# A hybrid decoder layer: softmax row factors of attention taken from TensorE transposes to a DMA round trip

## What is computed

```python
logits = where(mask, scores * 64 ** -0.5 + F[t] - F[s], -inf)
p = softmax(logits, axis=-1)          # row sum over the keys
out = einsum('bhqk,bkhd->bqhd', p, v)
```

## Time and profile before

| | |
|---|---|
| median of 3 runs | 1952.44 us (1950.23 to 1953.33) |
| profiled execution, its own time | 1954.57 us |
| its span | 1953.0 us, mean granted TensorE clock 0.994 |
| TensorE matmuls | 1915.2 us busy, 98% |
| TensorE weight loads | 1624.5 us, 83% |
| VectorE | 1124.6 us, 58% |
| ScalarE | 709.0 us, 36% |
| GpSimd | 435.1 us, 22% |
| DMA | 221.69 MB, mean 114 GB/s |

### The profile page before, as it was taken

The page is one execution under the profiler, slowest core; times in us unless marked ns, Lnnn a source line. Parts: engine busy times, 40 slices in busy tenths (PEclk is TensorE's granted clock), DMA queues, the critical chain, the costliest instruction groups (busy, mean ns, idle before and its releaser), DMA issues. The chain is left out here.

```text
span 1953.0 us, 30551 instructions
## 1 busy us (share of the span) xinstructions
PE 1915.2 (98%) x10560; PEld 1624.5 (83%) x10560; DVE 1124.6 (58%) x2142; ACT 709.0 (36%) x1090; POOL 435.1 (22%) x548
## 2 busy tenths in 40 slices
PE   8999999999999999999999999999999989999998
PEld 6878887888887888888888788888888878999997
DVE  5564235654244655646566665565655568777676
ACT  3121013021034554555555655455555541111110
POOL 2927940498000000000000000000000002222322
PEclk9999999999999999999999999999999999999999
DMA  7124225322432141241513515133142276555642
GB/s 191 67 88 118 86 86 194 65 108 107 131 118 94 49 129 63 71 120 48 138 57 91 182 50 139 56 88 109 48 136 66 88 258 215 165 173 170 173 118 87
DMA packets 104568, 221.69 MB, mean 114 GB/s; under 512 B 11000, under 2 KB 56744, under 8 KB 100904
## 3 DMA queue, kind: packets, MB, share of 16 engines
q1 hardware_dynamic: 90736, 161.41, 26.2%
q0 software_dynamic: 12608, 55.19, 10.3%
q10 hardware_dynamic: 1152, 4.19, 0.5%
HBM read 155.09 MB, written 65.08 MB: 113 GB/s over the span
## 5 line engine op out<-in xcount | busy, mean ns | idle before, releaser
L1441 PE MATMUL g_ps<-x_hi,w_lo 128*128 128x512 f32 x768 | 310.2, 404 | 0.0
L1441 PE MATMUL g_ps<-x_hi,w_hi 128*128 128x512 f32 x768 | 308.7, 402 | 0.0
L1355 DVE TENSOR_TENSOR pt_lo<-t_ps,pt_hi 128x512 fp32r<-128x512 f32 (+2 forms) x320 | 191.7, 607 | 133.9 <-ACT pt_hi L1263 132.1
L1441 PE MATMUL g_ps<-x_lo,w_hi 128*128 128x512 f32 x768 | 228.4, 411 | 4.0 <-PEq L1478 2.6
L695 PE MATMUL tile_ps<-x_hi,w_hi 128*128 128x512 f32 x736 | 228.4, 391 | 0.0
L695 PE MATMUL tile_ps<-x_lo,w_hi 128*128 128x512 f32 x736 | 226.7, 389 | 0.0
L695 PE MATMUL tile_ps<-x_hi,w_lo 128*128 128x512 f32 x736 | 226.6, 389 | 0.0
L1263 ACT ACTIVATE pt_hi<-t_ps 128x512 fp32r<-128x512 f32 (+2 forms) x320 | 170.4, 534 | 134.3 <-PE t_ps L1400 129.4
L1171 POOL DMA_DIRECT2D mixT<-y_out x63 | 33.8, 536 | 749.7 <-DVE y_out L1309 749.7
L1295 DVE CUSTOM_DVE_ANT_0 s_sb<-s_ps,f_row 128x512 f32<-128x512 f32 (+2 forms) x320 | 180.6, 604 | 18.6 <-PE s_ps L1389 17.9
L1400 PE MATMUL t_ps<-ident,s_sb 128*128 128x128 f32 x1088 | 171.7, 273 | 0.9 <-DVE pt_lo L1355 0.9
(11 more groups left out here) (288 smaller groups left out, 3574.0 us busy)
## 6 DMA issues: line engine op xcount, KB each, us to landing
w_lo_raw<-in_w_tiles SPq DMA_DIRECT2D x96, 512.0 KB, 3.6
gateT<-g_out SPq DMA_DIRECT2D x96, 256.0 KB, 3.0
gate<-gateT SPq DMA_DIRECT2D x64, 384.0 KB, 4.6
qkvT<-zout SPq DMA_DIRECT2D x24, 512.0 KB, 3.2
x_lo_raw<-in_xT SPq DMA_DIRECT2D x20, 512.0 KB, 8.6
silT<-zout SPq DMA_DIRECT2D x16, 512.0 KB, 2.6
k_ll<-qkvT POOLq DMA_DIRECT2D x16, 512.0 KB, 7.2
q_st<-qkvT POOLq DMA_DIRECT2D x16, 512.0 KB, 8.9
```

The lines of the kernel that those rows point to most:

```text
L1355: dve.tensor_tensor(pt_lo[part], t_ps[n % 2][:, 0:keys].rearrange("p (k q) -> p k q", q=P), pt_hi[part].bitcast(F32), ALU.subtract).then_i ...
L1441: mm = pe.matmul(g_ps[c][:], w[j % 2][:, k, :], x[:, k, c * BANK:(c + 1) * BANK], start=(r == 0), stop=(r == 3 * KT - 1))
```

## The change

`values` no longer transposes the reciprocals, and `o_ps` loses its second half. ScalarE instead writes the pair's two columns of `row_inv` to a DRAM row of 256 values (`factors_out`, at tile 2p+2 after the exp and ahead of `low_rows`; 128 runs of 8 bytes) and loads that row broadcast over 64 partitions into rows 64 to 127 of `y_out[p % 2]` (`factors_in`, at tile 2p+3 after the gate work). Both go over ScalarE's DMA queue. For pair 7 the store comes after the "end" gate work, the load between the rounding of k and of q; in the last head after the weights' rounding.

VectorE's `output` is cut in two: `add_rows` makes the sum into rows 64 to 127 of `o_low` at tile 2p+2, `output` multiplies it by the factors at tile 2p+4, ahead of the next pair's sum. `values` waits for the sum of the pair before. GpSimd's stores of the outputs move back by one against the next head's loads: pairs 0 to 4 before k and q, 5 after them, 6 and 7 after the forget row. Semaphores of the key and query splits are merged.

```diff
+            def factors_out(at, p):
+                act.wait_ge(inv_ready, at(8, p + 1))
+                act.dma_start(scr["inv"][bass.ds(at(8, p), 1)].rearrange("o (q a) -> q (o a)", a=2),
+                              row_inv[:, 2 * p:2 * p + 2]).then_inc(inv_stored, 16)
+
+            def factors_in(at, p):
+                if p >= 2:
+                    act.wait_ge(y_ready, at(8, p))
+                else:
+                    act.wait_ge(y_ready, at(8, 1))
+                act.wait_ge(inv_stored, at(128, 16 * (p + 1)))
+                act.dma_start(y_out[p % 2][HD:P], scr["inv"][bass.ds(at(8, p), 1)].partition_broadcast(HD)
+                              ).then_inc(inv_loaded, 16)
...
-            def split_kq(loaded):
+            def split_kq(loaded, between=None):
                 act.wait_ge(kq_loaded, loaded)
-                act.activation(k_hh[:], k_ll[:].bitcast(F32), ACT.Copy).then_inc(k_hi, 1)
+                act.activation(k_hh[:], k_ll[:].bitcast(F32), ACT.Copy).then_inc(kq_high, 1)
+                if between:
+                    between()
...
                     if t % 2 == 0 and t >= 2:
+                        factors_out(at, t // 2 - 1)
                         low_rows(at, t // 2 - 1)
+                    if t % 2 == 1 and t >= 3:
+                        factors_in(at, t // 2 - 1)
...
+            def add_rows(at, p):
+                dve.wait_ge(o_low_ready, at(8, p + 1))
+                dve.wait_ge(y_ready, at(8, p + 1))
+                dve.sem_inc(passed)
+                dve.tensor_tensor(o_low[HD:P], o_ps[0:HD, :], o_low[0:HD], ALU.add).then_inc(o_sum, 1)
+
             def output(at, p):
-                dve.wait_ge(o_low_ready, at(8, p + 1))
+                dve.wait_ge(o_sum, at(8, p + 2))
+                dve.wait_ge(inv_loaded, at(128, 16 * (p + 1)))
                 dve.wait_ge(y_free, at(8, p + 1))
                 y = y_out[p % 2]
-                dve.tensor_tensor(y[:], o_ps[0:HD, 0, :], o_low[:], ALU.add).then_inc(o_sum, 1)
-                dve.wait_ge(o_sum, at(8, p + 1))
-                dve.tensor_tensor(y[:], y[:], o_ps[0:HD, 1, :], ALU.mult).then_inc(y_ready, 1)
+                dve.tensor_tensor(y[0:HD].rearrange("d (a q) -> d a q", a=2),
+                                  o_low[HD:P].rearrange("d (a q) -> d a q", a=2),
+                                  y[HD:P].rearrange("d (q a) -> d a q", a=2), ALU.mult).then_inc(y_ready, 1)
...
                     if t % 2 == 0 and t >= 2:
-                        output(at, t // 2 - 1)
+                        if t >= 4:
+                            output(at, t // 2 - 2)
+                        add_rows(at, t // 2 - 1)
...
                 for j in splits("end", last):
                     split_w(at, j)
+                output(at, 6)
...
                     split_kq(at(1, 2))
+                add_rows(at, 7)
                 output(at, 7)
...
                 pe.wait_ge(t_lo, at(PT_USES, pieces_to(2 * p + 1) + 2))
-                if p:
-                    pe.wait_ge(y_ready, at(8, p))
+                pe.wait_ge(o_sum, at(8, p + 1))
...
-                pe.wait_ge(inv_ready, at(8, p + 1))
-                pe.sem_inc(passed)
-                for a in range(2):
-                    last = pe.transpose(o_ps[0:HD, 1, a * P:(a + 1) * P],
-                                        row_inv[:, 2 * p + a:2 * p + a + 1].broadcast_to([P, HD]), ident[:])
                 last.then_inc(o_full, 1)
```

More of the change, by code:

```diff
@@ L99, in __init__ @@
         self.g_out = [at(f"g_out{i}", 5, [P, BANK], skip=4 * i * BANK) for i in range(NCH)]
-        self.y_out = [at(f"y_out{i}", 5, [HD, 2 * P], skip=4 * (2 * BANK + i * 2 * P)) for i in range(2)]
+        self.y_out = [at(f"y_out{i}", 5, [P, 2 * P], skip=4 * (2 * BANK + i * 2 * P)) for i in range(2)]
         self.ln_g = at("ln_g", 5, [P, D])
@@ L1150, in _ @@
                         load_w((T_HALF + u) * P, u)
-            sp.wait_ge(y_ready, HEADS * 8)
+            sp.wait_ge(y_ready, HEADS * 8 + 1)
             row = (HEADS - 1) * HD + 2 * P
-            sp.dma_start(scr["mixT"][row:row + HD, 14 * P:], y_out[1][:]).then_inc(last_y_stored, 16)
+            sp.dma_start(scr["mixT"][row:row + HD, 14 * P:], y_out[1][0:HD]).then_inc(last_y_stored, 16)
         @block.gpsimd
@@ L1168, in store_y @@
             def store_y(h8, row, p):
[L1170 removed]
+                pool.wait_ge(y_ready, h8 + (p + 2))
                 pool.dma_start(scr["mixT"][bass.ds(row, HD), p * 2 * P:(p + 1) * 2 * P],
[L1172 removed]
+                               y_out[p % 2][0:HD]).then_inc(y_stored, 16)
                 pool.wait_ge(y_stored, h8 * 16 + 16 * (p + 1))
@@ L1179, in _ @@
             with pool.Fori(0, HEADS - 1) as h:
-                for p in range(6):
+                for p in range(5):
                     store_y(h * 8, h * HD + 2 * P, p)
@@ L1221, in low_rows @@
                 act.wait_ge(o_full, at(8, p + 1))
-                act.activation(o_low[:], o_ps[HD:P, 0, :], ACT.Copy).then_inc(o_low_ready, 1)
-            def split_kq(loaded):
-                act.wait_ge(kq_loaded, loaded)
-                act.activation(k_hh[:], k_ll[:].bitcast(F32), ACT.Copy).then_inc(k_hi, 1)
-                act.activation(q_tmp[HD:P], q_st[HD:P].bitcast(F32), ACT.Copy, scale=HD ** -0.5).then_inc(q_hi_tmp, 1)
-                act.activation(q_st[0:HD], q_st[0:HD].bitcast(F32), ACT.Copy, scale=HD ** -0.5).then_inc(q_hi, 1)
+                act.activation(o_low[0:HD], o_ps[HD:P, :], ACT.Copy).then_inc(o_low_ready, 1)
+            def factors_out(at, p):
[11 more added lines that the diff above has]
+            def split_kq(loaded, between=None):
+                act.wait_ge(kq_loaded, loaded)
+                act.activation(k_hh[:], k_ll[:].bitcast(F32), ACT.Copy).then_inc(kq_high, 1)
+                if between:
+                    between()
+                act.activation(q_tmp[HD:P], q_st[HD:P].bitcast(F32), ACT.Copy, scale=HD ** -0.5).then_inc(kq_high, 1)
+                act.activation(q_st[0:HD], q_st[0:HD].bitcast(F32), ACT.Copy, scale=HD ** -0.5).then_inc(kq_high, 1)
             def before(phase):
@@ L1413, in values @@
                     for j, pt in enumerate((pt_hi, pt_lo)):
-                        pe.matmul(o_ps[:, 0, q], v_st[:, k, :], pt[:, k, q], start=(k == 0 and j == 0),
-                                  stop=(k == last_key and j == 1))
-                pe.wait_ge(inv_ready, at(8, p + 1))
-                pe.sem_inc(passed)
-                for a in range(2):
-                    last = pe.transpose(o_ps[0:HD, 1, a * P:(a + 1) * P],
-                                        row_inv[:, 2 * p + a:2 * p + a + 1].broadcast_to([P, HD]), ident[:])
+                        last = pe.matmul(o_ps[:, q], v_st[:, k, :], pt[:, k, q], start=(k == 0 and j == 0),
+                                         stop=(k == last_key and j == 1))
                 last.then_inc(o_full, 1)
```

40 lines of the change are left out of this document (23 added, 17 removed).

## The result

The changed kernel takes **1973.57 us** (median of 4 runs, 1971.25 to 1974.37) against 1952.88 us for 4 runs of the kernel before. The ratio is 1.0096, 95% interval [1.0082, 1.0109]: slower by about 19 us, where 1938.4 us was forecast. It is outside the range and on the other side of no change. The profiled execution has a span of 1972.8 us, 19.8 us more than that of before, and a mean granted clock of 0.988 (0.994 before).

The account below looks back on a forecast made before the run. TensorE was taken to bound the attention stage, busy 99.87 of 100 us. Removing the transposes saves 14.0 us and all other terms cost 0: 1952.44 - 14.0 = 1938.4 us, range 1934.0 to 1945.0, forecast's chance 0.69.

Parts of the forecast that it names:

- The removed transposes: TensorE, attention stage: 128 transposes gone, 0.22 us a pair, 63 pairs counted, 14.0 us saved.
- rival (b): TensorE's step after the last value matmul shrinks too, saving 17.6 us in all: 1934.8 us; chance 0.08.
- VectorE's moved work: Sum and scaling at separate places in VectorE's order, the scaling where the engine waits anyway: cost 0.
- ScalarE's issues: Two DMA issues a pair on ScalarE, 128 in all, 0.46 us each, hidden beside its ACTIVATEs: cost 0.
- Rival (a): ScalarE's DMA issues do not hide and cost 5 us, leaving -9 us: 1943.4 us; chance 0.10.
- I take 2 to 3.5: cost 0: ScalarE's waits for the factor store: landing taken as 2 to 3.5 us after issue, so no TensorE stall.
- L: Time from the factor store's issue on ScalarE's queue to its landing; taken as 2 to 3.5 us.
- rival (c): Store lands late, ScalarE stands: 3 x (L - 4.0) + 8 x (L - 6.05), 1970.4 us at L = 8.4; chance 0.06.
- the part for pair 0: Pair 0's store in each of eight heads: TensorE stalls from L = 6.05 on, priced 8 x (L - 6.05).
- head 4 waits for x: Start of head 4: ScalarE begins x's split after a wait for TensorE, so no stall from L was priced there.
- no load waits longer: GpSimd's order with output stores 5 and 6 moved behind next-head loads lets no load wait longer: cost 0.
- counts nothing: Last head's eighth pair: stage ends with the chain over VectorE and SP, not TensorE, so no saving counted.

Follow-up runs that it names:

- e4: Changed kernel without factor stores, loads and their waits; the scaling multiplies the sum by itself: 1943.27 us, ratio 0.9932 to the kernel before.
- e5: Changed kernel with the two transposes of a pair put back, their result unused: 1992.31 us, ratio 1.0184 to the kernel before.
- e1: Changed kernel with pair 7's load and its wait moved behind the rounding of q: 1953.54 us, ratio 0.9989 to the kernel before.
- e6: Changed kernel with pair 7's load and its wait on GpSimd's queue, behind output store 6: 1960.84 us, ratio 1.0025 to the kernel before.
- e3: Changed kernel with pair 7's store issued at tile 15, right after pair 6's load: 1956.54 us, ratio 0.9998 to the kernel before.
- e2: Changed kernel with GpSimd's forget row load issued only after pair 7's store has landed: 1959.70 us, ratio 1.0017 to the kernel before.
- e8: Changed kernel with pair 7's store moved ahead of the end slot's gate work: 1952.53 us, ratio 0.9981 to the kernel before.
- e9: e8 with the forget row load held until pair 7's store has landed: 1949.80 us, ratio 0.9967 to the kernel before.
- e10: e8 with the forget row load held until pair 7's factors are loaded back: 1948.51 us, ratio 0.9969 to the kernel before.

## Why the prediction was wrong

**The removed transposes: right.** 0.22 us a pair. (The 390 ns that the prediction set beside it is given by the Trainium skill, page "VectorE: DVE Perf Modes", section "The three transpose paths", for a bf16 transpose of 128x128; these are float32 transposes of 64 output rows, so the trace does not test that figure.) The step from the last value matmul to the turn stays at 0.11 to 0.12 us, so rival (b) is out; e4 shows the 14.0 us in the total within its interval, e5 shows that it is there in the slow kernel too.

**VectorE's moved work: right inside a head.** Sum and scaling cost TensorE nothing in e1's and e4's first heads. At the end of a head the cost 0 of the last scaling held only as long as its factors were there: in e6 that scaling is where the loss sits.

**ScalarE's issues: right.** They take 0.34 and 0.48 us (0.46 forecast) and hide. The load's, at 1196.49 in tile 15 of head 4, lies under a gate activation that ends at 1197.03, and `pt_hi` follows at 1197.09:

```profile
1196.34 0.69 ACT L1218 ACTIVATE g_out<-g_ps,g_bias 128x512 f32<-128x512 f32 x1 [0.19 <-PE g_ps L1474]
1196.49 0.49 ACTq L1239 DMA_DIRECT2D y_out<-inv  x1
1197.09 0.60 ACT L1286 ACTIVATE pt_hi<-t_ps 128x512 fp32r<-128x512 f32 x1
```

Rival (a) is out; it holds only for a second issue right behind the first (e3).

**The step that failed: "I take 2 to 3.5: cost 0"** for L. In 44 of the 64 pairs it is right, and 12 others (pairs 1 and 3, once pair 0) take up to 5.5 us without ScalarE waiting for any of them. Source line 1230 shows all 64:

```profile
DMA to landing us min/median/max: 2.7/3.1/10.7
```

128 runs of 8 bytes into DRAM cost, at the median, no more than the 3.2 us of the earlier trace rows, and nothing near the 25 us that the prediction worked out from the Trainium skill's warning on strided copies (page "VectorE: DVE Perf Modes", section "The three transpose paths"). The page limits that warning to copies whose innermost destination stride is large; here the 256 values stand side by side in DRAM, so no run here tests it, and the prediction was wrong to let it speak for rival (c). But one pair in eight is not like the others. In heads 0 to 6 pair 7's store is issued 1.8 to 2.5 us after GpSimd's load of v and 1.2 to 1.9 after that of the forget row, 1.5 MB together, and it lands after 6.7 to 10.7 us. The prediction had the row that warned of it, the 8.4 us of the earlier trace rows, and answered it with "its own queue, on which nothing lies ahead". A queue of its own was no protection (DMA view under e2).

The mechanism was that of rival (c), given 0.06, and its price per head was good: for the starts of heads 5 to 7 it gives 3 x (L - 4.0) summed over L = 6.7, 9.3 and 7.5, that is 11.5 us, and the timeline has 12.3 (3.1, 5.4, 3.8). For head 4's start it was given nothing (below), and the part for pair 0 never came: its landings stay under 3.9 us, far from the 6.05 at which it would have begun. It erred in two more places:

- **"head 4 waits for x"** was taken as a shelter. The start of head 4 is the longest wait of all, 7.1 us at L = 10.7, as L - 4.0 would have it. Its first scores don't wait for x; and in e1, where x's split is what is late, that split stands behind the same landing in ScalarE's order. The three starts with 30 fills (heads 1 to 3) were protected from a wait for q, as said. Not from all of it: the fills need gate activations, and these and the exp stand behind the late rounding in ScalarE's order, so TensorE waits four times for 0.5 to 0.8 us between 733 and 978 us, 2.4 us together.
- **The clock was not priced.** At each late head start the granted clock was 0.50 for 3.4 to 10.2 us; the stretched steps add 9.7 us by the account (7.3 against e4) to the 19.4 us of the waits at the head starts. Without that term even the right L, with head 4 counted, would have given 1952.4 - 14.0 + 19.4 = 1957.8 us, well short of the 1973.57 measured; with the 9.7 of the clock and the 3.9 of the border it would be 1971.4.

**GpSimd's order, "no load waits longer":** not quite so. The output store ahead of the load of v now lands 11.1 to 12.0 us after its issue, where it was 7.5 to 8.5, and v is issued 99.9 to 100.6 us into heads 0 to 3, as before (99.7 to 100.6), though TensorE has been spared some 1.5 us by then (7 pairs); in e4 it is 98.8 to 99.3. Nobody waits for v, but its load and the forget row's come that much nearer to the store of the factors, and what those loads do to the store is what should have been asked.

**The last head, "counts nothing":** ScalarE waits there for 6.2 us before `y_hi`, and the border to the merge grows by 3.9 us. Of these, 2.4 come in e4 too, where no factor is transferred; what they are is open. The last head in e8 is 126.1 us against 122.7 in e4: 2.6 are steps at the half clock after its late start, 0.6 the border.

## What to carry to other kernels

In this kernel a small transfer through DRAM had the latency of the busy moment in which it was issued, not that of its empty queue: list the large loads of every other queue that are issued within a few microseconds of it, and price it at the worst landing shown. Then look at what stands behind its wait in program order, and move first the wait (e1), then the issue (e8), then the large load that can wait (e9, e10), before the idea itself is given up. Where TensorE is the bound, a wait of some microseconds can cost more than its length, since the clock may be low around it: a third more here.

## What the runs showed of the hardware

- A 1 KB store on ScalarE's queue moved no packet for 4.3 us while 1.43 MB of GpSimd's loads ran at a share of 101% of the 16 engines; a store on SP's queue, issued 1.25 us later, moved none before 1208.60 either. Undisturbed, the first packet came after 0.8 to 0.9 us (pairs 0, 2, 4, 5 and 6). Holding back 1 MB of the 1.5 MB cut the landing by 2.3 to 4.2 us (e2, heads 0 to 6).
- In e8 the store's last packet started by 2.8 us after the issue in six heads, and it landed after 5.9 to 6.9 us: a late landing without late packets.
- Two DMA issues in a row on ScalarE's queue took 0.48 + 0.41 us and held the next ACTIVATE for 0.69; single ones of 0.34 and 0.48 us lay under an ACTIVATE and cost nothing.
- Around the end of a wait of 2.9 us the granted clock was 0.50 for 6.8 us (1215.0 to 1221.8), and a matmul of 512 columns took 0.44 us of the stream in place of 0.24.
